# Two norms at block borders, computed by token halves instead of whole tiles

## The reference

```
x = x + rmsnorm(merged @ w_out, norm_mix_post)      # border 1: "wout" -> "mixpost"
h = rmsnorm(x, norm_ffn_pre)                        #           -> "ffnpre0" -> first products of the FFN
f = conv_ffn(h, ffn_w_up, ..., ffn_w_down)
x = x + rmsnorm(f, norm_ffn_post)                   # border 2: "down0" -> "ffnpost"
h = rmsnorm(x, fox_norm)                            #           -> "fox" -> first products of the attention
rmsnorm(x, g) = x * rsqrt(mean(x*x over the 1024 channels) + 1e-6) * g     # one mean per token
```

## Time and profile before

| | |
|---|---|
| three runs | 2219.13, 2219.86, 2220.64 us (median 2219.86) |
| the profiled execution | 2220.61 us, of which the span of its instructions is 2218.8 us |
| PE busy | 2180.9 us (98%) |
| DVE, ACT, POOL busy | 1197.1, 902.1, 947.9 us |
| mean granted TensorE clock | 0.997 |
| border 1, from the last product of `wout` to the sum for `ffnpre0` | 446.5 to 477.8 us |
| border 2, from the last product of `down0` to the sum for `fox` | 820.6 to 856.2 us |

### The profile page before, as it was taken

How to read it: one execution, slowest core, us unless ns; L and a number is a source line. 1 busy time by engine, 2 the same in 40 slices (tenths; PEclk the granted TensorE clock), 3 DMA queues, 4 the chain that set the end, 5 groups by cost and what they waited for, 6 DMA issues and landing times.

```text
span 2218.8 us, 26264 instructions
## 1 busy us (share of the span) xinstructions
PE 2180.9 (98%) x10482; PEld 1784.7 (80%) x10482; DVE 1197.1 (54%) x1714; ACT 902.1 (41%) x1384; POOL 947.9 (43%) x727
## 2 busy tenths in 40 slices
PE   9999999999999999999999999999999999999998
PEld 6887788867888877777888888887888888888887
DVE  5766423579765016676566662166766424666502
ACT  5214432354343234576533342254445334343322
POOL 5334434535545444321544444443222244444442
PEclk9999999999999999999999999999999999999999
DMA  4221222323333322210333333322111233333332
GB/s 173 74 72 62 77 81 92 110 69 95 96 101 93 95 90 79 74 57 30 113 96 95 95 94 101 95 92 73 55 53 48 62 95 95 97 99 100 90 96 90
DMA packets 58057, 191.74 MB, mean 86 GB/s; under 512 B 6464, under 2 KB 8656, under 8 KB 57936
## 3 DMA queue, kind: packets, MB, share of 16 engines
q1 hardware_dynamic: 57936, 190.07, 27.6%
HBM read 187.95 MB, written 2.10 MB: 86 GB/s over the span
## 4 chain that ended last, share of the span: by engine, by line
PE 88%; DVE 7%; ACT 2%; DMA 2%; issue 1%; POOL 0%; ACTq 0%; DVEq 0%; SPq 0%
PE ps L575 25%; PE ps L576 25%; PE ps L577 25%; PE ps L1056 2%; DMA RAW<-weights 2%; PE ps L628 1%; PE ps L629 1%; PE ps L630 1%; PE ps L952 1%; DVE TURNED L1596 1%; PE ps L943 1%; PE ps L1007 1%; PE ps L686 1%; DVE CV L1599 1%; PE ps L976 1%
## 5 line engine op out<-in xcount | busy, mean ns | idle before, releaser
L567 POOL TENSOR_TENSOR WLO<-RAW,WHI 128x512 fp32r<-128x512 f32 (+1 forms) x723 | 947.7, 1336 | 1245.5 <-ACT WHI L1153 1245.1
L1153 ACT ACTIVATE WHI<-RAW 128x1024 fp32r<-128x1024 f32 (+2 forms) x375 | 373.7, 1000 | 672.0 <-DMA RAW<-weights 484.9
L575 PE MATMUL ps<-HH,WHI 128*128 128x512 f32 x1200 | 474.3, 395 | 8.3 <-DVE HL L1599 3.7
L577 PE MATMUL ps<-HH,WLO 128*128 128x512 f32 x1200 | 468.0, 390 | 0.0
L576 PE MATMUL ps<-HL,WHI 128*128 128x512 f32 x1200 | 467.9, 390 | 0.0
L1599 DVE SCALAR_TENSOR_TENSOR CV<-U,PAR,CV 128x512 f32<-128x512 f32 x264 | 280.1, 1081 | 8.9 <-ACT CV L1382 4.2
L575 PEld LDWEIGHTS ps<-HH,WHI 128*128 128x128 f32 x1200 | 225.4, 188 | 61.9 <-issue 7.1
L576 PEld LDWEIGHTS ps<-HL,WHI 128*128 128x128 f32 x1200 | 225.5, 188 | 47.6 <-issue 2.4
L577 PEld LDWEIGHTS ps<-HH,WLO 128*128 128x128 f32 x1200 | 225.4, 188 | 47.2
L575 PE MATMUL ps<-ACTH,WHI 128*128 128x512 f32 (+1 forms) x550 | 209.8, 381 | 0.0
L576 PE MATMUL ps<-ACTL,WHI 128*128 128x512 f32 (+1 forms) x550 | 209.6, 381 | 0.0
(11 more groups left out here) (319 smaller groups left out, 3299.8 us busy)
## 6 DMA issues: line engine op xcount, KB each, us to landing
RAW<-weights SPq DMA_DIRECT2D x300, 512.0 KB, 3.5
RAW<-weights SPq DMA_DIRECT2D x48, 384.0 KB, 3.0
RAW<-weights SPq DMA_DIRECT2D x27, 256.0 KB, 2.6
X<-xT SPq DMA_DIRECT2D x4, 512.0 KB, 6.5
outT<-X SPq DMA_DIRECT2D x8, 256.0 KB, 2.2
RESET<-resets SPq DMA_DIRECT2D x1, 512.0 KB, 10.9
CS<-rope SPq DMA_DIRECT2D x1, 512.0 KB, 3.4
M8F<-masks SPq DMA_DIRECT2D x1, 448.0 KB, 10.1
```

Source lines behind the costliest of these rows:

```text
L567: pool.tensor_tensor(WLO[:, slot, w], RAW[:, slot, w], WHI[:, slot, w].bitcast(F32), ALU.subtract).then_inc(w_lo, 1)
L575: pe.matmul(out, wh, hh, start=first, stop=False)
L577: return pe.matmul(out, wl, hh, start=False, stop=last)
L1153: act.activation(WHI[:, slot, 0:cols], RAW[:, slot, 0:cols], ACT.Copy).then_inc(w_hi, 1)
```

## The change

Both borders are described by a small class `Border` and written by common functions.

1. The last output tiles of the product stage (tiles 6 and 7 of `wout`, tile 7 of `down0`) are computed twice with 256 columns each: all of them for tokens 0 to 255, then all for tokens 256 to 511 (`split_groups`). In the second pass, after slice 4 of its first tile, stand the two half-size sum matmuls of the first half.
2. `keep_clock` is gone from both borders, `stats_in_two` too.
3. ACT: half squares, the root of the first half, the squares of the second half, four steps (H and square) on tiles 0 to 3 of the first half, the root of the second half, then four steps on tiles 0 to 3 of the second half and four on whole tiles 4 to 7.
4. DVE: copies and sums by halves; the copy of the last tile's second half waits for its square and stands ahead of the first step; then four half steps, a wait for the second root, four half steps, four whole steps.
5. PE: the next stage's first two chunks (slices 0 to 3) are worked for the first token half, then for the second; the sum matmuls of the second half stand behind the first products of the first half.
6. Casts of weights: the last two or three chunks of the next stage's head are cast after steps 3 and 5 (border 1) or 1, 3 and 5 (border 2), one chunk before the border.

```diff
-            stats_in_two("mixpost", 8)
-            keep_clock(24)
+            split_groups(MIXPOST, *M_)
...
+            def split_groups(b, hi, lo):
+                for n, half in enumerate(TOKEN_HALVES):
+                    for i, j in enumerate(b.groups):
...
+                                mm = split_mm(ps[:, bank, half], WHI[:, c % RING, w], WLO[:, c % RING, w],
+                                              hi[k][:, half], lo[k][:, half], k == 0, k == tiles - 1)
+                                if n and i == 0 and k == 4:
+                                    half_stats(b, 0)
...
+STEPS = ([(j, half) for half in TOKEN_HALVES for j in range(4)] + [(j, slice(0, T)) for j in range(4, KD)])
...
+            (PE, first products of the FFN)
+                    for n, half in enumerate(TOKEN_HALVES):
+                        for at in range(2):
+                            for name in UP0_HEAD:
...
+                                    pe.wait_ge(MIXPOST.lo, n * 4 + k + 1)
+                                    mm = split_mm(ps[:, BANK[name], half], ...)
+                                if n:
+                                    mm.then_inc(lin_done, 1)
+                                elif at == 0 and name == UP0_HEAD[1]:
+                                    half_stats(MIXPOST, 1)
...
+            (ACT, border)
+                def step(s):
+                    j, half = STEPS[s]
+                    act.wait_ge(b.x, s + 1)
+                    act.activation(hi[j][:, half], X[:, j, half], ACT.Copy, scale=par(gain, j)).then_inc(b.hi, 1)
+                    if s >= 2:
+                        act.wait_ge(b.nsum, s - 1)
+                    act.activation(SQ[:, j % 2, half], X[:, j, half], ACT.Square).then_inc(b.nsq, 1)
+                    if s in late:
+                        casts(late[s])
+                for i in range(m):
+                    half_square(0, i)
+                half_root(0)
+                for i in range(m):
+                    half_square(1, i)
+                for s in range(4):
+                    step(s)
+                half_root(1)
+                for s in range(4, len(STEPS)):
+                    step(s)
...
+            (DVE, border)
+                dve.wait_ge(b.rstd, 1)
+                half_copy(1, m - 1)
+                run(0, 4)
+                dve.wait_ge(stat_done, STAT_AT[b.following])
+                dve.memset(SUMSQ[:, TOKEN_HALVES[1]], 0.0).then_inc(cleared, 1)
+                dve.wait_ge(cleared, STAT_AT[b.following] + 1)
+                scale_known(b.site)
+                run(4, len(STEPS))
...
-            root("mixpost", D, RSTD)
-            for j in range(KD):
-                act.wait_ge(x_done, j + 1)
-                h_tile(j, j % 2, "ffnpre0", "ffnpre0")
-                if j == 1:
-                    casts(chunk_of("gate0.0"))
+            casts(chunk_of("gate0.0", 1))
+            border(MIXPOST, "ffnpre0", {3: chunk_of("gate0.0", 2), 5: chunk_of("gate0.0", 3)})
...
+            casts(chunk_of("fv0.0", 0))
+            border(FFNPOST, "fox", {1: chunk_of("fv0.0", 1), 3: chunk_of("fv0.0", 2), 5: chunk_of("fv0.0", 3)})
```

More of the change, by code:

```diff
@@ L458, in on_chip_model, with __init__ @@
         tap, conv_done, act_done, ffn_dve, acts = (sem(n) for n in ("tap", "conv_done", "act_done", "ffn_dve", "acts"))
-        post_dve = sem("post_dve")
+        class Border:
+            def __init__(self, name, stage, groups, site, following, banks):
+                self.stage, self.groups, self.site, self.following, self.banks = stage, groups, site, following, banks
+                self.lin, self.drain, self.sq, self.sum, self.stat, self.ln, self.rstd = (
+                    sem(f"{name}_{n}") for n in ("lin", "drain", "sq", "sum", "stat", "ln", "rstd"))
+                self.clear, self.scaled, self.x, self.hi, self.lo, self.nsq, self.nsum = (
+                    sem(f"{name}_{n}") for n in ("clear", "scaled", "x", "hi", "lo", "nsq", "nsum"))
+        MIXPOST = Border("mixpost", "wout", (6, 7), "mixpost", "ffnpre0", (2, 3))
+        FFNPOST = Border("ffnpost", "down0", (7,), "ffnpost", "fox", (2,))
         a_s, a_m, a_e, a_p, a_t, a_pt, a_o, a_hi, a_rs = (
@@ L572, in _, with split_mm @@
         def _(pe):
[L573 to L577, removed]
+            def split_mm(out, wh, wl, hh, hl, first, last, joins=False):
+                pe.matmul(out, wh, hh, start=first, stop=False, skip_group_check=joins)
+                pe.matmul(out, wh, hl, start=False, stop=False, skip_group_check=joins)
+                return pe.matmul(out, wl, hh, start=False, stop=last, skip_group_check=joins)
             seen = [0]
@@ L590, in bank_free, with part @@
                     pe.wait_ge(drained, PRIOR[name])
-            def part(name, at, hi, lo, ready=None, tiles=None):
+            def part(name, at, hi, lo, ready=None, tiles=None, joins=False):
                 c, first, blocks, col = PARTS[name][at]
@@ L636, in stats, with half_stats @@
                 pe.matmul(ps[:, 7, :], ones, SUMSQ[:, :], start=True, stop=True).then_inc(stat_done, 1)
[L638 to L648, removed]
+            def half_stats(b, n):
+                half, m = TOKEN_HALVES[n], len(b.groups)
+                if m > 1:
+                    pe.wait_ge(b.sum, (n + 1) * (m - 1))
+                else:
+                    pe.wait_ge(sumsq, SQ_AT[b.site] + KD - m + 2)
+                pe.matmul(ps[:, HALF_SUM[n], half], ones, SUMSQ[:, half], start=True, stop=False)
+                pe.wait_ge(b.sq, (n + 1) * m)
+                mm = pe.matmul(ps[:, HALF_SUM[n], half], ones, SQ[:, 1, half], start=False, stop=True)
+                mm.then_inc(stat_done if n else b.stat, 1)
@@ L650, in h_ready, with following_stats @@
+            def following_stats(b):
+                pe.wait_ge(b.nsum, len(STEPS))
+                pe.matmul(ps[:, 7, :], ones, SUMSQ[:, :], start=True, stop=True).then_inc(stat_done, 1)
             def h_ready(site):
@@ L914, in ffn @@
                     group(f"val{f}.{q}", *h)
[L915 removed]
+                for j in range(KD if f == 1 else KD - 1):
                     group(f"down{f}.{j}", *ACTS[f], (acts, 1 + KF * f) if j == 0 else None)
             ffn(0)
[L919 to L920 removed]
+            split_groups(FFNPOST, *ACTS[0])
             def causal_scores(B, pairs, full):
@@ L1977, in into_x @@
                     add_square(j, j % 2, site)
[L1979 to L1992, removed]
+            border(MIXPOST)
             ffn(0)
-            into_fb("down0", "ffnpost")
-            post_norm("ffnpost", "fox", KD)
+            border(FFNPOST)
             def row_maxima(n, r, B):
```

198 lines of the change are left out of this document (154 added, 44 removed).

## The result

| | before | after |
|---|---|---|
| median of 8 runs each, same chip | 2220.6 us (2218.39 to 2222.76) | 2227.68 us (2226.08 to 2229.55) |
| ratio to before | | 1.0032, 95% interval 1.0021 to 1.0043 |
| profiled execution, span | 2220.61, 2218.8 | 2226.78, 2225.0 |
| border 1: T, T1, sum | 446.53, –, 477.79 | 447.08, 448.58, 481.58 |
| border 2: T, T1, sum | 820.63, –, 856.19 | 824.39, 826.12, 864.01 |

The change costs 7.1 us; the forecast was 2228.9 us, slower by more than 0.2%, and the whole interval lies above 0.2%. In the column after, T1 is read from the trace as the end of the last split product, and T is T1 less the 1.50 and 1.73 us that were forecast for splitting. From T to the sum it is now 34.5 and 39.6 us, where it was 31.26 and 35.56: +3.2 and +4.1.

The account below looks back on a forecast made before the run. PE's products bound the kernel, and at the borders PE waits for DVE. Border 1 at +3.9 and border 2 at +5.1 us made +9.0: 2229.6 on the profiled execution, 2228.9 us as median; range 2221 to 2234.

Parts of the forecast that it names:

- signs: Expected in the new trace, among others: PE idle about 3 us before the second half's first product, last wait at slice 5.
- Split products, +1.5 and +1.73: End of the product stage: half-size products and two half sums there end it 1.5 and 1.73 us later.
- Half sum late: Rival: a late square on ACT delays the half sum and split products, up to 1 us each; no chance of its own.
- Early start: Next stage's first product on PE: T1 + 3.3 us at border 1, a gain of 3.8 us; 5.1 at border 2.
- Second root, the part that decides: ACT's root behind step 3, a cast and two table loads: ready T1 + 11.8 and 14.4; DVE idle 3.8 at border 1.
- Collisions: DVE's half steps beside POOL's splitting: three, one at border 1 and two at border 2, 2.3 us each.
- collisions vanish: Rival: half operations slip between POOL's pieces; borders +1.6 and +0.5 us, 2222 us in all; chance 0.14.
- Second half: DVE's work after the second root: low part 9 at T1 + 26.0 and 28.5, including 0.5 us for a cast at border 1.
- The clock, 0: PE's idle stretches at the borders: clock drops cost 0, as PE finds the lost work again in its next wait.
- The higher price that the prediction set beside its own: PE's idle gaps: each costs its lost work in full, up to four times 1.7 = 6.8 us; unabsorbed clock's chance 0.17.
- Early start wins: Rival, DVE's queue between steps 3 and 4: with stall and collisions gone, -2.0 and -3.1 us, 2214.8 us; chance 0.09.
- Sum: Both borders together: 3.9 + 5.1 = +9.0 us, giving 2228.9 us.

Follow-up runs that it names:

- b: The changed kernel with the Ln table of the second root loaded ahead, in ACT's idle time before the last half square: 2225.61 us, ratio to before 1.0025.
- d: The changed kernel with two Copy activations in place of Ln and Exp in the second root, so without its table loads: 2224.45 us, ratio to before 1.0017.
- c: The changed kernel with POOL splitting three chunks of the heads in 8 columns instead of 512: 2221.48 us, ratio to before 1.0005.
- a: The changed kernel with unread bf16 filler matmuls in PE's two idle stretches of each border: 2228.02 us, ratio to before 1.0033.
- h: The changed kernel with each head's last chunk cast after step 9, not 5, and fv0's second after step 2, not 1: 2224.13 us, ratio to before 1.0018.
- j: The changed kernel with both the edits of c and d: 2219.33 us, ratio to before 0.9993.
- f: The kernel before with the head's chunk cast after the sixth tile, not the second, at both borders: 2216.61 us, ratio to before 0.9987.
- g: f with the casts ahead of the last square moved behind it and the Ln table load to its front: 2220.62 us, ratio to before 1.0003.
- i: f with the Ln table load moved ahead of the casts of the product stage's last tile: 2215.16 us, ratio to before 0.9977.

## Why the prediction was right

The mechanism was as forecast: three collisions, a late second root, and drops of the clock without a price. Two sizes, two of the signs and the point at which the early start should win were not. The number looks better than it was: the runs of the kernel before had their median at 2219.86 us at the forecast and at 2220.6 beside the changed kernel, so of the 1.9 us by which the cost was overrated (9.0 for 7.1) 0.7 were made good by chance.

- *Split products, +1.5 and +1.73.* From the first split product to T1: 436.2 to 448.58 is 12.4 us, where the same work took 435.65 to 446.53, 10.9; at border 2, 16.7 for 15.0. As worked out.
- *Half sum late.* The rival's cause is absent: at 443.76 and 819.14 PE did not stop.
- *Early start.* First product at T1 + 3.25 and 3.26 (3.3).
- *Second root, the part that decides.* Ready at T1 + 11.7 and 13.8 (11.8 and 14.4); low part 4 at T1 + 13.8 and 15.9 (13.9 and 16.5). b and d confirm it as a cost. One of my signs held only in part: PE was to be idle for about 3 us before the second half's first product, and was for 3.21 us at border 2 but for 1.15 at border 1, since at half clock it finished the first half 12.7 us after T1, not 11.1. With the filler it was through at T1 + 11.0.
- *Collisions.* Three, at the places named, 1.95 to 2.0 us each above 0.48 + 0.42, not 2.3; c gives 1.9 and 3.9 us for one and two. A fourth, on a half-size sum at 441.43 (1.31 us), lies beside the products and costs nothing. The rival "collisions vanish" fell. The case is that of the Trainium skill, page "SBUF — State Buffer", section "Who interferes with whom": it says that a DVE instruction with two SBUF inputs contends with a GpSimd instruction that reads SBUF, over a port pair that is an exclusive lock. The trace agrees as far as it goes: beside POOL's splitting a scaling or low part of DVE takes 1.40 us at half size and 1.79 at whole size, for 0.48 and 0.75, so 0.9 to 1.1 us are added at either length.
- *Second half.* Low part 9 at T1 + 25.35 and 27.4, predicted 26.0 and 28.5: the mis-sized terms are the collision and the 0.5 for the cast behind step 5, which fell into the collision (DVE's operation that waited for ACT there started at 464.92, beside POOL's splitting from 464.57 on, and would have been held anyway). This is the 0.7 and 1.1 us by which the sums came earlier (T + 34.5 and 39.6 for 35.2 and 40.7). At border 2 two collisions are in it.
- *The clock, 0.* It fell as expected, to half; a shows that the drops behind the early starts cost nothing, and the rows above that the later ones cost 0.1 us at most. The higher price that the prediction set beside its own (each gap paid in full, up to 6.8 us) did not come true here. It can elsewhere: in h one drop came behind the last wait and cost 1.6 us, the 1.7 at which the prediction had priced it. But one of my signs failed: at border 1 the last wait of PE is for slice 3 of the second half (469.19), not slice 5. In the 3.3 us at clock 0.51 behind it PE worked at half pace and came to slice 5 at 474.00, just as its low part (473.93) was there. What I had booked as a wait was slow work that ended at the same moment, which is luck: a little more of it would have been paid. The rest, 474.00 to 481.58, is the 33 matmuls of the sum (7.58 us).
- *Early start wins.* The prediction named a stall under 1.5 us as the point from which this rival wins. For the stall gone and the collisions left it forecast 2226.8, still slower; d is nearest to that (stall 0.58 and 0.94 us) and took 2224.45. For both gone it forecast -2.0 and -3.1 us and 2214.8; j is nearest to that and measured about 0 and -1.4 us and 2219.33, level with before. The point of decision was wrong in what it took the early start for: it left out that a shorter stall uncovers the splitting beneath it (1.40 us for 0.42 in d), so in j one collision is still there at each border.
- *Sum.* +7.3 us at the borders for 9.0; 7.1 in the runs. The two spans differ by 6.2: T came 0.55 us later in the profile of the changed kernel, and the stretch behind the last sum was 1362.6 us in before's and 1361.0 in after's. In the profiles of all twelve kernels it lies between 1359.4 and 1363.0 without any order by edit. Its cause is open, and the lowest of them is f's, whose gain the borders left unexplained.

## What to carry to other kernels

Starting a stage earlier by halves pays only if the second half's inputs are ready when the first half's work is used up: count, in the written order of each engine, what stands ahead of them (here a cast and two table loads), and lay out the list of the second half as carefully as that of the first. A stall on one engine can be the cover of another's work. Take it away and expect a part of the gain back as a collision, so move such work to where the waiting engine has slack rather than to where it merely comes later. Before a border is rebuilt, try the small moves in it: one cast and one table load moved in the old order gave 5 us, where the rebuilt border cost 7.

## What had not been expected of the hardware

The same short stops of PE (0.77 and 1.5 to 1.6 us behind the filler) let the granted clock fall to half in some profiles (0.53 at 832.20 in f, 0.50 at 458.70 in g) and not in others (1.00 at 830.10 in i). What a drop costs depends on what PE still has to wait for behind it: nothing that could be seen behind the early starts of the changed kernel, 0.76 us in f, where one wait of 0.42 us was left to take up a part, and 1.6 us in h, where none was.

An `ACT_TABLE_LOAD` of 1.28 us was followed by its activation 0.01 to 0.02 us later (458.54 + 1.28, then 459.84). Between the Exp of the second root (459.84) and the Copy and the Square behind it (461.33 and 461.75) the trace has no load at all.

A low clock can also hide a wait. In the changed kernel PE had no idle time ahead of slice 5, because half pace (0.51 from 470.40 to 473.70) stretched its work until the low part was there. That no idle time is recorded is therefore no proof that an input was early.
